# The mask matmul of the latent-attention scores, contracted over 64 rows instead of 128

## The reference

```
def chunk_mask(blk, seq_len):
    q_pos = blk * Q_BLOCK + jnp.arange(Q_BLOCK)
    k_pos = jnp.arange(seq_len)
    return (k_pos[None, :] // CHUNK) <= (q_pos[:, None] // CHUNK)      # CHUNK = 64, Q_BLOCK = 128
...
    def block(args):
        qn, qp, blk = args
        sc = (jnp.einsum('bqhd,bkhd->bhqk', qn, k_nope)
              + jnp.einsum('bqhr,bkr->bhqk', qp, k_pe)).astype(jnp.float32) * scale
        p = masked_softmax(sc, chunk_mask(blk, s)[None, None])
        return jnp.einsum('bhqk,bkhe->bqhe', p.astype(v.dtype), v)
```

## Time and profile before

| what | value |
|---|---|
| time, median of 3 runs | 1795.26 us (1791.67 to 1796.55) |
| time of the profiled execution | 1795.26 us |
| its span, first to last instruction | 1793.4 us |
| mean granted TensorE clock | 0.996 of full speed |
| instructions | 23164 |
| matmuls, and as many weight loads | 8992 |
| of these, mask matmuls of `score` steps | 64 |

### The profile page before, as it was taken

The page is one execution under the profiler, slowest core; times in us unless marked ns, Lnnn a source line. Parts: engine busy times, 40 slices in busy tenths (PEclk is TensorE's granted clock), DMA queues, the critical chain, the costliest instruction groups (busy, mean ns, idle before and its releaser), DMA issues.

```text
span 1793.4 us, 23164 instructions
## 1 busy us (share of the span) xinstructions
PE 1768.7 (99%) x8992; PEld 1493.5 (83%) x8992; DVE 1118.0 (62%) x1895; ACT 791.2 (44%) x1419; POOL 136.3 (8%) x133
## 2 busy tenths in 40 slices
PE   9999999999999999999999999999999999999998
PEld 7798788888888888877888888888888888888886
DVE  4578644344346766796764754656879776366375
ACT  5563432232235455544532432456766544144144
POOL 2003200000004100002000000023010110000000
PEclk9999999999999999999999999999999999999999
DMA  5212333332333122122323333332011133333331
GB/s 164 74 48 64 98 94 95 105 94 94 94 100 100 60 65 66 60 65 77 94 95 98 102 94 94 95 86 74 26 53 43 59 94 94 96 104 95 95 118 70
DMA packets 128330, 152.33 MB, mean 85 GB/s; under 512 B 9339, under 2 KB 102045, under 8 KB 128221
## 3 DMA queue, kind: packets, MB, share of 16 engines
q1 hardware_dynamic: 128060, 150.78, 27.2%
q10 hardware_dynamic: 160, 0.07, 0.0%
HBM read 148.59 MB, written 2.10 MB: 84 GB/s over the span
## 4 chain that ended last, share of the span: by engine, by line
PE 91%; DVE 3%; ACT 2%; issue 2%; POOL 1%; DMA 0%; SPq 0%; ACTq 0%; DVEq 0%; POOLq 0%
PE bk L1747 22%; PE bk L1749 22%; PE bk L1748 22%; PE bk L1776 5%; PE bk L1778 5%; PE bk L1777 5%; PE bk L1752 4%; PE bk L1848 1%; PE bk L1814 1%; POOL FS L2223 1%; DVE XT L1917 1%; PE bk L1821 1%; PE bk L1835 1%; DVE WL L1905 1%; PE bk L1836 1%
## 5 line engine op out<-in xcount | busy, mean ns | idle before, releaser
L1747 PE MATMUL bk<-R,WH 128*128 128x512 f32 x1764 | 691.6, 392 | 5.7 <-DVE R L1911 3.1
L1749 PE MATMUL bk<-R,WL 128*128 128x512 f32 x1764 | 687.5, 390 | 0.0
L1748 PE MATMUL bk<-R,WH 128*128 128x512 f32 x1764 | 687.1, 390 | 0.0
L1905 DVE TENSOR_TENSOR WL<-RAW,WH 128x1024 fp32r<-128x1024 f32 (+4 forms) x278 | 343.8, 1237 | 490.7 <-ACT WH L2086 490.1
L2086 ACT ACTIVATE WH<-RAW 128x1024 fp32r<-128x1024 f32 (+4 forms) x278 | 288.0, 1036 | 603.9 <-PE bk L1749 546.4
L1747 PEld LDWEIGHTS bk<-R,WH 128*128 128x128 f32 x1764 | 331.7, 188 | 74.2 <-issue 6.2
L1749 PEld LDWEIGHTS bk<-R,WL 128*128 128x128 f32 x1764 | 331.4, 188 | 69.7
L1748 PEld LDWEIGHTS bk<-R,WH 128*128 128x128 f32 x1764 | 331.7, 188 | 67.4
L1776 PE MATMUL bk<-WH,R 128*128 128x512 f32 (+4 forms) x528 | 188.4, 357 | 0.0
L1778 PE MATMUL bk<-WL,R 128*128 128x512 f32 (+4 forms) x528 | 179.8, 341 | 0.0
L1777 PE MATMUL bk<-WH,R 128*128 128x512 f32 (+4 forms) x528 | 179.6, 340 | 0.0
(11 more groups left out here) (156 smaller groups left out, 1625.8 us busy)
## 6 DMA issues: line engine op xcount, KB each, us to landing
RAW<-in_ffn_w_up_dram SPq DMA_DIRECT2D x176, 256.0 KB, 3.1
RAW<-in_ffn_w_down_dram SPq DMA_DIRECT2D x44, 512.0 KB, 3.7
RAW<-in_w_gate_dram SPq DMA_DIRECT2D x44, 256.0 KB, 2.8
RAW<-in_w_up_dram SPq DMA_DIRECT2D x44, 256.0 KB, 3.1
RAW<-in_w_down_dram SPq DMA_DIRECT2D x22, 512.0 KB, 3.7
RAW<-in_da_w_qkv_dram SPq DMA_DIRECT2D x32, 256.0 KB, 2.9
RAW<-in_w_out_dram SPq DMA_DIRECT2D x8, 512.0 KB, 3.8
RAW<-in_da_w_qkv_dram SPq DMA_DIRECT2D x8, 512.0 KB, 3.5
```

Source lines behind the costliest of these rows:

```text
L1747: e.matmul(dst, lh, rh, start=start, stop=False)
L1748: e.matmul(dst, lh, rl, start=False, stop=False)
L1749: return e.matmul(dst, ll, rh, start=False, stop=stop)
L1905: e.tensor_tensor(low, RAW[:, r, 0:m], high.bitcast(F32), ALU.subtract).then_inc(on["wlo_dve"], 1)
```

## The change

The fourth matmul of a `score` step reads the first 64 rows of both constants instead of all 128. The corner scores get -2^100 instead of -2^101, which is as good a mask. Nothing else is changed.

```
                     e.matmul(dst[:, 0:nk], qh, KT[r, st.kidx, 0:nk], start=True, stop=False)
                     e.matmul(dst[:, 0:nk], ql, KT[r, st.kidx, 0:nk], start=False, stop=False)
                     e.matmul(dst[:, 0:nk], qh, KT[r, st.kidx + 1, 0:nk], start=False, stop=False)
-                    e.matmul(dst[:, nk - P:nk], UPPER, MASK_H, start=False, stop=True).then_inc(on["score_pe"], 1)
+                    e.matmul(dst[:, nk - P:nk], UPPER[0:64, :], MASK_H[0:64, :], start=False, stop=True).then_inc(on["score_pe"], 1)
```

## The result

The changed kernel takes 1812.01 us (median of 4 runs, 1810.58 to 1812.75), the kernel before in the same runs 1794.3 us. The ratio is 1.0098, with a 95% interval of 1.0081 to 1.0115: 1% slower, 17.7 us. Forecast were 18.3 us on top of 1795.3, or 1813.6 us. Of the 1.6 us between forecast and result, 1.0 us is the base, since the kernel before now has a median of 1794.3.

A forecast was written before the change was run, and what follows sets the result against it. TensorE was taken to bound the kernel and the score stretch, with DVE not far behind. Borders of 20.3 us less 2.0 us covered by waits gave +18.3 us on 1795.3 us: 1813.6 us, range 1808 to 1818.

The forecast's parts named there:

- The border: At the lone 64-row mask of each score unit: TensorE stands still on both sides, 0.33 us, or 0.28 with 128 keys.
- Going in: From 512 columns into the mask: its load starts 0.31 us after the matmul ahead; cost 0.19 us.
- Going out: Behind the mask: the next load waits and loses its cover; cost 0.14 us.
- forecast sum: Borders over 64 score units: 15.8 us for 48 wide ones plus 4.5 us for 16 with 128 keys, 20.3 us.
- The cover: Score stretch, mostly 1280 to 1297 us: TensorE's waits for DVE or ACT absorb 2.0 us of delay; ends 0 and 5.0.
- A: Score stretch: nothing is covered, waits for DVE move along with TensorE; 1815.6 us, up to 1817; chance 0.25.
- B: At the mask: a lone row tile costs only one of the two crossings; 1804 to 1807 us; chance 0.07.
- C: At the mask: the change does nothing, 64 rows are treated as 66 and 96 are; 1795 us; chance 0.05.
- D: At the mask: faster, the next load needn't wait for the mask to start; 1788 to 1792 us; chance 0.03.
- signs to look for: Profile of line 1838: load 0.31 us after 512 columns, PEld standing still in all 64 cases, stretch about 173 us.

The follow-up runs named there:

- corner: Kernel before, with the mask matmul using 64 weight and 64 moving columns, writing only the masked corner, issued second in the score step: 1793.85 us, ratio 1.0001.
- rows96: Kernel before, with the mask matmul contracting 96 rows instead of 128: 1794.11 us, ratio 1.0001.
- rows65: Kernel before, with the mask matmul contracting 65 rows instead of 128: 1793.11 us, ratio 0.9999.
- no_mask: Kernel before, without the mask matmul of the score steps: 1791.16 us, ratio 0.9984.
- upper_half: Changed kernel, with the mask matmul contracting rows 64 to 127 instead of 0 to 63: 1813.01 us, ratio 1.0111 to the kernel before.
- rows32: Changed kernel, with the mask matmul contracting only rows 0 to 31: 1812.96 us, ratio 1.0115 to the kernel before.
- rows64_twice: Changed kernel, with its 64-row mask matmul issued twice in a row: 1820.33 us, ratio 1.0149 to the kernel before.
- four_borders: Changed kernel, with the second score matmul (line 1836) also contracting only rows 0 to 63: 1847.53 us, ratio 1.0298 to the kernel before.
- middle_borders: Kernel before, 128-row mask kept, with only the second score matmul (line 1836) contracting rows 0 to 63: 1812.19 us, ratio 1.0109.
- flag_rows: Kernel before, without mask matmul; the mask rides in four more rows of the first score matmul, written by GpSimd copies: 1796.88 us, ratio 1.0020.
- flag_rows_2: As flag_rows, but the planner doesn't count the GpSimd copies, so other engines keep the order of the kernel before: 1800.15 us, ratio 1.0041 to that kernel.
- flag_rows_3b: As flag_rows_2, but the new constants lie in their own tensor behind all others, with their own DMA: 1789.34 us, ratio 0.9978 to the kernel before.

## Why the prediction was right

**The border.** The rule that made the sum was read off two-tile borders 600 us earlier, and a lone 64-row matmul follows it. Going in behind 512 columns: 0.31 us forecast, 0.32 measured. Going out, from load to load: 0.11 + 0.15 = 0.26 us by rows 8 and 9, and 0.25 to 0.26 us measured. Over a whole unit, from the matmul ahead of the mask to the third behind it, the two traces differ by 0.31 to 0.35 us for 45 of the 48 wide units and 0.26 to 0.29 us for 14 of the 16 narrow ones (0.33 and 0.28 forecast). With their means, 48 x 0.332 + 16 x 0.275 gives 20.3 us, the forecast sum.

**The cover.** Forecast 2.0 us. PEld's waits for other engines in the stretch fall from 5.0 us to 2.6 us, of which these are the largest in the changed kernel (compare rows 11):

```profile
PEld bk L1835 <- DVE PT L1911: 0.9, 1, 0.9
PEld bk L1752 <- DVE R L1911: 0.6, 1, 0.6
PEld bk L1747 <- DVE PT L1911: 0.6, 2, 0.3
```

The wait of 0.9 us stayed whole: it hangs on TensorE's own earlier work (in the kernel before, at 1297.29 us, PEld waits for a copy that DVE makes right behind a `max`, and that `max` had itself waited for a mask of line 1838). Laid side by side matmul by matmul, the two traces give 18.8 us in the stretch: 20.3 us of borders, about 3 us given back by waits, and some 1.5 us that the sum hadn't.

**What the sum hadn't** is the clock. In the changed kernel the granted clock fell once in the stretch, at 1301.8 us, for 3.4 us:

```profile
1301.80:1305.20 3.40, 3.40 (x11) 2.67 (x11) 1.61 (x5) 1.90 (x4) 0.00 (x0) 0.50 0.02 5
```

```profile
1302.97 0.63 PE L1748 MATMUL bk<-R,WH 128*128 128x512 f32 x1
1303.40 0.63 PE L1749 MATMUL bk<-R,WL 128*128 128x512 f32 x1
1303.83 0.63 PE L1747 MATMUL bk<-R,WH 128*128 128x512 f32 x1
```

512 columns take 0.43 us there instead of 0.23, six times: 6 x 0.20 = 1.2 us, and the transposes ahead of them lost some 0.3 us more. So the forecast put the cover one us too small and left out a term of one and a half, and the two nearly cancelled. That the sum came within half a us of the stretch is luck to that extent (the borders alone came out as forecast). In the whole profiled execution it is 17.3 us, since the fall at 71.5 us cost the kernel before, and it alone, 1.5 us.

**The rivals.** A (nothing is covered) missed by the 3 us of waits, though its 1815.6 us lie near and the time alone would hardly decide between it and the forecast; the waits do. B (one crossing only) is out by the timelines, which show both. C (no change) is out as such, but it is true one row further up, at 65. D (a load pulled ahead) is out: in all 64 units the mask's load comes 0.20 to 0.33 us after the start of the matmul ahead of it. The Trainium skill's rule that a change of tiling mode drains TensorE, page "TensorEngine Tiling (Array Packing)", section "Tiling Modes", is borne out by the 0.36 us standing still above, for row tilings. The corner mask, whose weights have 64 columns, ran without it; whether such a matmul is a column tiling for the chip no run shows.

**What was off in the signs to look for.** I had said that PEld would stand still for "issue" in all 64 cases. The profile lists 32 of them, 9.8 us, those with 384 and 512 keys. With 128 and 256 keys the mask's load follows 0.07 to 0.15 us behind the modelled end of the load ahead, and the profile doesn't list gaps so short. Only the distance of the starts tells it.

## What to carry to other kernels

A matmul with 64 or fewer rows between full ones is dearer than a full one, by a third of a microsecond here: TensorE stands still on both sides and the loads lose their cover. Take the contraction to more than 64 rows (65, 96 and 128 took the same time here), or put the small matmuls side by side, so that one pair of borders serves many (the second mask added 0.11 us). Time saved on the leading engine of a balanced stretch can be worth less than time added to it: of some 7 us of slots taken away 2.9 came back as time, while of 20 us of borders added 18 did.

## What the runs showed of the hardware that was not expected

**The step is at 64 rows, and it is sharp.** 65, 96 and 128 rows: 1793 to 1794 us. 64 rows, in the lower or the upper half, and 32 rows: 1812 to 1813 us.

**With borders the clock fell more often.** In the profiled executions the kernel before, rows96, rows65, no_mask and corner had no fall of the granted clock in this stretch; the changed kernel, upper_half, rows32 and rows64_twice had one each, of 3.4 us; four_borders had about 30 us. It isn't a rule without exception: middle_borders had none, and flag_rows, without any border, had one at 1254 us. Over all executions the mean clock was 0.995 to 0.998 for the kernel before, 0.995 to 0.996 for the changed one, and 0.986 to 0.990 for four_borders, where the effect is clear. Falls also come without any lone border, as the one at 71.5 us in the kernel before, and those of flag_rows_2 and flag_rows_3b just ahead of the stretch. What exactly lets the clock fall stays open.

**Where operands start matters a little.** With R, KT and PT 64 bytes further, the most frequent matmul takes 396 instead of 392 ns, and the kernel 11 us longer (1800.15 against 1789.34 us, on two chips; the ratios to the kernel before are 1.0041 and 0.9978). For this matmul only R can be the one; moving it alone wasn't tried.
